# Products that nobody reads beside the attention's late units, and the norm's sums in two PSUM banks

## The chip, the cores and the metric

The kernel runs on one core of a Trainium2 chip. The metric is the device time of one execution in microseconds (us). Its engines are called by the profile's names: PE (TensorE's matmuls), PEld (TensorE's weight loads, which overlap the matmuls), DVE (VectorE), ACT (ScalarE), POOL (GpSimd) and SP (the queue that issues most DMAs).

## What is computed

One step of a one-layer encoder: a SwiGLU block, a mixer, another SwiGLU block, each followed by a layer norm. The mixer adds two branches that do not depend on each other. One is sparse attention (8 heads of 64, each query takes its 256 best keys). The other is a gated recurrence (4 heads with a 128 x 128 state), whose output is normalised by its root mean square. Cut to what matters here:

```python
S, o = lax.scan(step, S0, (q, k, v, logf))              # the recurrence, 4 heads of 128
s = einsum(q, k) * A_HEAD_DIM ** -0.5 - slopes * dist    # attention, masked to the chosen keys
o_a = einsum(softmax(s), v)
on = orec * lax.rsqrt(mean(square(orec), -1) + RMS_EPS) * gn     # the norm over each head
ob = on * silu(bg)
mixed = (sigmoid(ga) * (o_a @ wa) + sigmoid(gb) * (ob @ wb)) @ wo
```

## The kernel before, in words

The kernel has three phases, one after the other: the first SwiGLU block with the index search and the projections (to about 1460 us), `mixers` (to about 1777 us) and `back` (output projections, second SwiGLU block, last norm). Between them all engines meet at a barrier. The change is in `mixers` alone.

In `mixers` the attention is cut into units: 10 blocks of queries by 8 heads give 80 units. A unit has three steps on TensorE. `scores` ("S") multiplies the queries with the keys into one of two banks `ps_s`, in pieces of at most 512 keys. `turn` ("T") transposes the softmax weights into one of two banks `ps_t`, four tiles of 128 keys to a bank. `values` ("V") multiplies them with the values. Between S and T, VectorE takes the maximum (L2028) and ScalarE the exponential (L1934), and between T and V ScalarE copies the turned weights out of PSUM (L1949, L1953). "X" (`turn_out`) turns the output of a finished block. The later blocks have more keys: 656, 784, 912 and 1040 for the last four.

The order of all this is one list, `order`, made by `pass_order`, and every engine walks it (ScalarE with S put behind T). S runs two units ahead of T (`LOOK = 2`). The recurrence's steps ("k", "v", "u", "a", "o"; 14 of each) are dealt out between the units of the first 62% of the list. Its state product "u" writes the bank `ps_u`, which VectorE adds to the state, with `sum_done` counting. After the last step of the recurrence comes its norm, four heads. For each: "q" squares the output (ScalarE), "n" sums the squares over partitions by a product with a matrix of 1/128 (TensorE, L1914, three chunks of 384, 384 and 304 columns) and takes the root (ScalarE, L1989), "r" takes the reciprocal and multiplies (VectorE, L2082 and L2084, one chunk each), and "g" multiplies with the gate (VectorE, L2088).

PSUM has 8 banks, and all are in use: two `ps_s`, two `ps_t`, `ps_o`, and three `ps_n`. The recurrence uses these last three as `ps_kv`, `ps_ao` and `ps_u`; `ps_u` is `ps_n[2]`. In the norm, chunk i of each head uses `ps_n[i]`.

In the list, the last "u" stands at position 222. From the first S behind position 228 (the scores of unit 51) there follow 29 S, 31 T, 32 V, 4 n and 5 X.

Of the kernel before, what the change touches and what calls it, by code (L numbers as in the profile page):

```python
# [19 lines left out]
ACT = mybir.ActivationFunctionType  # L20
AX = mybir.AxisListType

P = 128
# [1682 lines left out]
def mixers(c, dram):  # L1706
# [14 lines left out]
    for b in [0, 1, "meta", "s"] + list(range(2, NB)):  # L1721
# [4 lines left out]
        else:  # L1726
            at, keys = SCORE_AT[b]
# [5 lines left out]
    order = pass_order(len(blocks), Recurrence.NRT)  # L1733
# [15 lines left out]
    with ExitStack() as st:  # L1749
# [9 lines left out]
        v_tok, k_hi, k_lo = c.v_tok, c.ka_hi, c.ka_lo  # L1759
# [10 lines left out]
        peak, peak_s, bias = sb("peak", [P, 2, 3]), sb("peak_s", [P, 2, 3]), sb("bias", [P, 2])  # L1770
# [10 lines left out]
        gn, eps, ones = sb("gn", [P, BH]), sb("eps", [P, 1]), sb("ones", [P, P])  # L1781
# [4 lines left out]
        r = Recurrence(c, dram, c.decay, ps_n, sb)  # L1786
# [9 lines left out]
        with nc.Block() as block:  # L1796
# [19 lines left out]
            @block.tensor  # L1816
            def _(pe):
                def cache():
                    pe.wait_ge(cache_in, 32)
                    for m, (src, dst, rows) in enumerate(prep):  # L1820
                        if m >= 2:
                            pe.wait_ge(kv_done, m - 1)
                        pe.transpose(ps_t[m % 2][0:rows, 0:P], src, c.ident[:]).then_inc(kv_mm, 1)

                def scores(n):
                    b, h = units[n]
                    q0, m, keys, prompt, _ = blocks[b]
                    hi, lo = (k_hi, k_lo) if prompt else (ks_hi, ks_lo)
                    if h == 0:
                        pe.wait_ge(crossed, 2 * b + 2)  # L1830
                        if not prompt:
                            pe.wait_ge(k_crossed, 4)
                    for i, (k0, w) in enumerate(pieces(keys)):
                        x = piece_at[n] + i
                        if x >= 2:
                            pe.wait_ge(peak_done, x - 1)

                        product_stacked(pe, ps_s[x % 2][:, 0:w], stack[:, b % 2, h, :], hi[:, h // 4, k0:k0 + w],
                                        lo[:, h // 4, k0:k0 + w]).then_inc(s_mm, 1)

                def turn(n):
                    b, h = units[n]
                    m, keys = blocks[b][1], blocks[b][2]
                    pe.wait_ge(exp_done, n + 1)
                    if n == 0:
                        pe.wait_ge(kv_done, len(prep) + 1)
                    tiles = (keys + P - 1) // P
                    for j, k in enumerate(range(0, tiles, 4)):
                        x = turn_at["T", n] + j
                        if x >= 2:  # L1850
                            pe.wait_ge(t_done, x - 1)
                        for i in range(k, min(k + 4, tiles)):
                            r = min(P, keys - i * P)
                            mm = pe.transpose(ps_t[x % 2][0:r, (i - k) * QB:(i - k) * QB + m],
                                              prob[0:m, n % (LOOK + 1), i * P:i * P + r], c.ident[0:m, 0:m])
                        mm.then_inc(t_mm, 1)

                def values(n):
                    b, h = units[n]
                    q0, m, keys, prompt, _ = blocks[b]  # L1860
                    tiles = (keys + P - 1) // P
                    if h == 0 and b >= 1:
                        pe.wait_ge(otok_done, b)
                    vt = v_tok if prompt else cv_tok
                    kv = slice(DH * (h // 4), DH * (h // 4) + DH)
                    for i in range(tiles):
                        if i % 4 == 0:
                            pe.wait_ge(t_done, turn_at["T", n] + i // 4 + 1)
                        r = min(P, keys - i * P)
                        mm = pe.matmul(ps_o[0:m, h * DH:(h + 1) * DH], prob_t[0:r, n % 2, i, 0:m], vt[0:r, i, kv],  # L1870
                                       start=i == 0, stop=i == tiles - 1)
                    mm.then_inc(o_mm, 1)

                def turn_out(b):
                    m = blocks[b][1]
                    x = turn_at["X", b]
                    pe.wait_ge(otok_done, b + 1)
                    pe.wait_ge(t_done, x - 1)
                    for j in range(4):
                        mm = pe.transpose(ps_t[x % 2][:, j * QB:j * QB + m], o_tok[0:m, j * P:(j + 1) * P], c.ident[0:m, 0:m])  # L1880
                    mm.then_inc(t_mm, 1)

                for what, n in order:
                    if what == "c":
                        cache()
                    elif what == "k":
                        r.turn_keys(pe, n)
                    elif what == "v":
                        r.turn_values(pe, n)
                    elif what == "u":  # L1890
                        r.update(pe, n)
                    elif what == "a":
                        r.attend(pe, n)
                    elif what == "o":
                        r.read(pe, n)
                    elif what == "S":
                        scores(n)
                    elif what == "T":
                        turn(n)
                    elif what == "V":  # L1900
                        values(n)
                    elif what == "X":
                        turn_out(n)
                    elif what == "n":
                        if n == 0:
                            pe.wait_ge(cst, 2)
                            pe.wait_ge(r.out_done, r.NRT)
                            pe.wait_ge(r.vtok_done, r.NRT)
                            pe.wait_ge(r.sum_done, r.NRT)
                        for i, (t0, w) in enumerate(CHUNKS):  # L1910
                            pe.wait_ge(sq_done, 3 * n + i + 1)
                            if n >= 1:
                                pe.wait_ge(rms_done, 3 * n + i - 2)
                            pe.matmul(ps_n[i][:, 0:w], ones[:], sq[:, i, 0:w], start=True, stop=True).then_inc(r_mm, 1)  # L1914

            @block.scalar
            def _(act):
# [38 lines left out]
                for what, n in act_order(order):  # L1956
                    if what == "k":
                        r.keep_keys(act, n)
                    elif what == "v":
                        r.keep_values(act, n)  # L1960
                    elif what == "q":
                        for i, (t0, w) in enumerate(CHUNKS):
                            if n == 0:
                                act.wait_ge(r.out_done, r.NRT)
                            else:
                                act.wait_ge(r_mm, 3 * n + i - 2)
                            act.activation(sq[:, i, 0:w], rq[:, n, t0:t0 + w], ACT.Square).then_inc(sq_done, 1)
                    elif what == "Q":
                        make_stack(n)
                        if n == 1:  # L1970
                            act.wait_ge(kv_done, len(prep) + 1)
                            for g_ in range(2):
                                act.activation(ks_hi[halves[g_], g_, :], ks_t[halves[g_], :], ACT.Copy).then_inc(khi_done, 1)
                    elif what == "S":
                        softmax(n)
                    elif what == "T":
                        keep_turned(n)
                    elif what == "X":
                        q0, m = blocks[n][0:2]
                        x = turn_at["X", n]  # L1980
                        act.wait_ge(t_mm, x + 1)
                        act.activation(c.aq[:, :, q0:q0 + m], ps_t[x % 2][:].rearrange("p (j q) -> p j q", j=4)[:, :, 0:m],
                                       ACT.Copy).then_inc(t_done, 1)
                    elif what == "n":
                        for i, (t0, w) in enumerate(CHUNKS):
                            act.wait_ge(r_mm, 3 * n + i + 1)
                            if n >= 1:
                                act.wait_ge(on_done, 3 * n + i - 2)
                            act.activation(rms[:, i, 0:w], ps_n[i][:, 0:w], ACT.Sqrt, bias=eps[:]).then_inc(rms_done, 1)  # L1989

            @block.vector
            def _(dve):
# [503 lines left out]
```

## Time and profile before

| | us |
|---|---|
| median of 3 runs | 2855.16 (2853.48 to 2855.99) |
| the profiled execution | 2865.82, its span 2864.1 |
| PE busy in the span | 2702.6 (94%) |
| PEld busy | 2611.5 (91%) |
| DVE, ACT, POOL busy | 1351.5, 695.7, 466.4 |
| mean granted clock of TensorE | 0.967 of 2.4 GHz |

PE's busy time counts matmuls whose ends are modelled and overlap, so the start-to-start times of a timeline tell more of its pace than the durations do. The last matmul of unit 79 ends at 1775.0 us of the span and the phase's last instruction, the copy behind the last X, at 1776.7.

### The profile page before, as it was taken

Reading aid. Unit: us, or ns where it says so; the run is one execution under the profiler, and the core shown is the slowest. Engines: PE = TensorE matmul, PEld = TensorE weight load, DVE = VectorE, ACT = ScalarE, POOL = GpSimd, SP = SyncE. Lnnn points to the kernel's source line nnn. Section 1 sums busy time; section 2 is a strip of 40 time slices with the busy share of each in tenths; the row PEclk is TensorE's granted clock in tenths of the full one; section 3 lists DMA queues with packets and bytes.
Section 4 is the critical chain, followed back from the end, with each engine's and each line's share of the span. In section 5 each row is a group of like instructions: output and inputs, shape, how many; then the busy total and the mean of one; then the engine's idle time right before and its main releaser. Section 6 shows DMA issues by size and latency. Waiting matters only on the chain. (4 is left out here: it accounts for less than half of the span.)

```text
span 2864.1 us, 41380 instructions
## 1 busy us (share of the span) xinstructions
PE 2702.6 (94%) x16384; PEld 2611.5 (91%) x16384; DVE 1351.5 (47%) x2834; ACT 695.7 (24%) x1162; POOL 466.4 (16%) x151
## 2 busy tenths in 40 slices
PE   8999999999987899999989997899999999999996
PEld 7999999999977789999978986898799999999995
DVE  3333333333353679999436664555633333333336
ACT  3111111111044443222525664101511111111102
POOL 1211111111110011222100000211121111111112
PEclk9999999999998899999999978999999999999998
DMA  4111111111012012222230001521011111111101
GB/s 150 45 44 44 44 44 44 44 44 44 17 37 69 20 30 52 91 94 65 76 108 2 8 1 46 174 90 39 30 59 44 44 44 44 44 44 44 44 15 61
DMA packets 144811, 149.11 MB, mean 52 GB/s; under 512 B 20240, under 2 KB 131440, under 8 KB 144576
## 3 DMA queue, kind: packets, MB, share of 16 engines
q1 hardware_dynamic: 141248, 134.45, 15.3%
q10 hardware_dynamic: 3456, 13.17, 1.1%
q8 instruction: 75, 1.23, 0.2%
q14 instruction: 32, 0.26, 0.0%
HBM read 123.82 MB, written 23.79 MB: 52 GB/s over the span
## 5 line engine op out<-in xcount | busy, mean ns | idle before, releaser
L477 DVE TENSOR_TENSOR ffn_prod<-ffn_gate,ffn_psu 128x384 f32<-128x384 f32 x132 | 69.5, 526 | 798.5 <-ACT ffn_gate L387 793.7
L67 PE MATMUL ixp_ps<-h_hi,ixp_hi 128*128 128x384 f32 (+1 forms) x1032 | 342.8, 332 | 29.0 <-ACT y L879 11.5
L387 ACT ACTIVATE ffn_gate<-ffn_psg 128x384 f32<-128x384 f32 x132 | 61.8, 468 | 1258.5 <-PE ffn_psu L69 1258.5
L67 PE MATMUL ffn_psd<-ffn_hid_hi,ffn_dn_hi 128*128 128x384 f32 (+1 forms) x1056 | 354.5, 336 | 12.7 <-DVE y L502 10.9
L502 DVE TENSOR_TENSOR y<-y,ffn_psd 128x384 f32<-128x384 f32 (+1 forms) x480 | 250.9, 526 | 218.1 <-PE ffn_psd L69 218.1
L67 PE MATMUL ffn_psg<-h_hi,ffn_up_hi 128*128 128x384 f32 (+1 forms) x1056 | 345.7, 327 | 8.2 <-DVE ffn_up_lo L402 6.5
L69 PE MATMUL ffn_psd<-ffn_hid_hi,ffn_dn_lo 128*128 128x384 f32 (+1 forms) x1056 | 344.1, 326 | 0.0
L68 PE MATMUL ffn_psd<-ffn_hid_lo,ffn_dn_hi 128*128 128x384 f32 (+1 forms) x1056 | 344.1, 326 | 0.0
L67 PE MATMUL ffn_psu<-h_hi,ffn_up_hi 128*128 128x384 f32 (+1 forms) x1056 | 344.0, 326 | 0.0
L68 PE MATMUL ffn_psg<-h_lo,ffn_up_hi 128*128 128x384 f32 (+1 forms) x1056 | 343.2, 325 | 0.0
L69 PE MATMUL ffn_psu<-h_hi,ffn_up_lo 128*128 128x384 f32 (+1 forms) x1056 | 343.0, 325 | 0.0
L69 PE MATMUL ffn_psg<-h_hi,ffn_up_lo 128*128 128x384 f32 (+1 forms) x1056 | 342.5, 324 | 0.0
L68 PE MATMUL ffn_psu<-h_lo,ffn_up_hi 128*128 128x384 f32 (+1 forms) x1056 | 342.1, 324 | 0.0
L68 PE MATMUL ixp_ps<-h_lo,ixp_hi 128*128 128x384 f32 (+1 forms) x1032 | 340.0, 329 | 0.0
L69 PE MATMUL ixp_ps<-h_hi,ixp_lo 128*128 128x384 f32 (+1 forms) x1032 | 339.0, 328 | 0.0
L406 POOL TENSOR_TENSOR ffn_dn_lo<-ffn_dn_raw,ffn_dn_hi 128x2048 fp32r<-128x2048 f32 x22 | 101.7, 4624 | 911.8 <-ACT ffn_dn_hi L380 911.8
L402 POOL TENSOR_TENSOR ffn_up_lo<-ffn_up_raw,ffn_up_hi 128x2048 fp32r<-128x2048 f32 x42 | 194.3, 4628 | 332.1 <-ACT ffn_up_hi L374 332.1
L67 PEld LDWEIGHTS ixp_ps<-h_hi,ixp_hi 128*128 128x128 f32 x1032 | 197.8, 192 | 30.9 <-issue 22.0
L67 PEld LDWEIGHTS ffn_psd<-ffn_hid_hi,ffn_dn_hi 128*128 128x128 f32 x1056 | 198.7, 188 | 28.4 <-DVE y L502 18.3
L67 PEld LDWEIGHTS ffn_psg<-h_hi,ffn_up_hi 128*128 128x128 f32 x1056 | 198.7, 188 | 9.1 <-DVE ffn_up_lo L402 6.7
L860 POOL TENSOR_TENSOR ixp_lo<-ixp_raw,ixp_hi 128x1024 fp32r<-128x1024 f32 x43 | 106.5, 2479 | 589.0 <-ACT ixp_hi L855 589.0
L68 PEld LDWEIGHTS ffn_psd<-ffn_hid_lo,ffn_dn_hi 128*128 128x128 f32 x1056 | 199.5, 189 | 0.3
(302 smaller groups left out, 4955.2 us busy)
## 6 DMA issues: line engine op xcount, KB each, us to landing
ffn_dn_raw<-in_ffn_wd SPq DMA_DIRECT2D x22, 1024.0 KB, 4.8
ffn_up_raw<-in_ffn_wg SPq DMA_DIRECT2D x20, 1024.0 KB, 5.4
ffn_up_raw<-in_ffn_wu SPq DMA_DIRECT2D x20, 1024.0 KB, 7.8
ixp_raw<-in_w_in SPq DMA_DIRECT2D x39, 512.0 KB, 3.8
spill<-y ACTq DMA_DIRECT2D x15, 536.0 KB, 2.7
mo_sig<-spill SPq DMA_DIRECT2D x32, 192.0 KB, 4.0
spill<-ix_stage ACTq DMA_DIRECT2D x9, 536.0 KB, 2.7
y<-y_spill SPq DMA_DIRECT2D x1, 4288.0 KB, 15.1
```

Of the source, the lines that this page charges most:

```text
L67: pe.matmul(out, w_hi, x_hi, start=first, stop=False)
L68: pe.matmul(out, w_hi, x_lo, start=False, stop=False)
L69: return pe.matmul(out, w_lo, x_hi, start=False, stop=last)
L387: act.activation(self.gate[:, k % 2, 0:w], self.ps_gate[k % banks][:, 0:w], ACT.Silu).then_inc(self.silu_done, 1)
L402: eng.tensor_tensor(self.up_lo[:, j], self.up_view(j), self.up_hi[:, j].bitcast(F32), ALU.subtract).then_inc(self.up_lo_done, 1)
L406: pool.tensor_tensor(self.dn_lo[:], self.dn_raw[:], self.dn_hi[:].bitcast(F32), ALU.subtract).then_inc(self.dn_lo_done, 1)
L477: dve.tensor_tensor(self.prod[:, k % 2, 0:w], self.gate[:, k % 2, 0:w], self.ps_up[k % banks][:, 0:w], ALU.mult).then_inc(self.prod_done, 1)
L502: dve.tensor_tensor(y, y, self.ps_dn[o % 2][:, 0:w], ALU.add).then_inc(self.y_done, 1)
L860: pool.tensor_tensor(self.lo[b], self.raw[:, n % 2], self.hi[b].bitcast(F32), ALU.subtract).then_inc(self.lo_done, 1)
```

## The change

Behind the recurrence, each S and each T of the attention gets three products ahead of it: 128 x 128 weights and 512 columns out of the keys, written into the recurrence's bank `ps_u`, which nobody reads any more. This holds for list positions above 228: 29 S and 31 T, so 60 times three products. The first seven of the 60 also wait until VectorE has read the last state product. The bank is thereby taken from the norm, whose chunks now use `ps_n[0]` and `ps_n[1]` in turn: chunk x waits until ScalarE's root of chunk x - 2 is done, where it had waited for chunk x - 3.

```diff
-                for what, n in order:
+                last_update = order.index(("u", r.NRT - 1))
+
+                def keep_warm():
+
+                    for _ in range(3):
+                        pe.matmul(r.ps_u[:], k_hi[:, 0, 0:P], k_hi[:, 0, 0:512], start=True, stop=True)
+
+                for at, (what, n) in enumerate(order):
+                    if at > last_update + 6 and what in "ST":
+                        if at < last_update + 20:
+                            pe.wait_ge(r.sum_done, r.NRT)
+                        keep_warm()
                     if what == "c":
                         cache()
...
                         for i, (t0, w) in enumerate(CHUNKS):
-                            pe.wait_ge(sq_done, 3 * n + i + 1)
-                            if n >= 1:
-                                pe.wait_ge(rms_done, 3 * n + i - 2)
-                            pe.matmul(ps_n[i][:, 0:w], ones[:], sq[:, i, 0:w], start=True, stop=True).then_inc(r_mm, 1)
+                            x = 3 * n + i
+                            pe.wait_ge(sq_done, x + 1)
+                            if x >= 2:
+                                pe.wait_ge(rms_done, x - 1)
+                            pe.matmul(ps_n[x % 2][:, 0:w], ones[:], sq[:, i, 0:w], start=True, stop=True).then_inc(r_mm, 1)
...
-                            act.activation(rms[:, i, 0:w], ps_n[i][:, 0:w], ACT.Sqrt, bias=eps[:]).then_inc(rms_done, 1)
+                            act.activation(rms[:, i, 0:w], ps_n[(3 * n + i) % 2][:, 0:w], ACT.Sqrt, bias=eps[:]).then_inc(rms_done, 1)
```

## Rows read from the trace of the kernel before

**Rows 1.** The page: the clock granted to TensorE in 40 slices of 71.6 us.

```profile
PEclk9999999999998899999999978999999999999998
```

**Rows 2.** Windows behind the recurrence: stretch, length, busy PE PEld DVE ACT POOL, clock, DMA.

```profile
1616.45:1655.50 39.05, 36.67 (x255) 32.44 (x255) 30.94 (x82) 30.32 (x68) 0.00 (x0) 1.00 0.00 1
1655.50:1675.80 20.30, 20.00 (x82) 18.07 (x81) 10.97 (x29) 8.57 (x22) 0.00 (x0) 0.50 0.00 1
...
1699.60:1709.70 10.10, 10.10 (x36) 8.49 (x37) 2.12 (x10) 5.66 (x14) 0.00 (x0) 0.50 0.01 2
...
1723.30:1726.90 3.60, 3.60 (x18) 3.46 (x19) 3.09 (x8) 1.78 (x4) 0.00 (x0) 0.53 0.00 0
...
1736.50:1746.50 10.00, 9.77 (x45) 8.40 (x42) 2.35 (x12) 3.26 (x7) 0.00 (x0) 0.53 0.00 0
...
1616.45:1772.80 156.35, 143.07 (x870) 125.37 (x870) 87.81 (x238) 88.94 (x191) 0.00 (x0) 0.86 0.00 1
```

**Rows 3.** TensorE's waits in that stretch: who for whom, us, times, longest.

```profile
PEld mx_s L809 <- DVE mx_peak L2028: 13.7, 16, 2.1
PE mx_s L809 <- DVE mx_peak L2028: 9.9, 13, 1.8
PE mx_t L1854 <- ACT mx_prob_t L1949: 1.5, 6, 0.3
PE mx_t L1854 <- ACT aq L1982: 1.5, 3, 0.7
```

**Rows 4.** Timeline of PE at full clock, units of 784 keys: start us, us, instruction.

```profile
1649.00 0.44 PE L809 MATMUL mx_s<-ka_hi,mx_stack 128*128 128x392 f32 x1
...
1652.66 0.63 PE L1880 MATMUL mx_t<-ident,mx_o_tok 128*128 128x128 f32 x4 [0.27 <-ACT mx_prob_t L1949]
```

**Rows 5.** The same at half clock: one whole cycle of a unit.

```profile
1660.26 0.69 PE L809 MATMUL mx_s<-ka_hi,mx_stack 128*128 128x392 f32 x1
...
1666.43 0.69 PE L809 MATMUL mx_s<-ka_hi,mx_stack 128*128 128x392 f32 x1
```

**Rows 6.** Timeline of PE, full clock: three 456-column products, then the turn.

```profile
1679.55 0.37 PE L810 MATMUL mx_s<-ka_lo,mx_stack 128*128 128x456 f32 x1
...
1680.17 0.93 PE L1854 MATMUL mx_t<-ident,mx_prob 128*128 128x128 f32 x7
```

**Rows 7.** Timeline of DVE: one unit's cycle with a piece of the norm.

```profile
1626.19 2.55 DVE L2082 RECIPROCAL y<-y 128x384 f32<-128x384 f32 x1
...
1630.35 2.55 DVE L2082 RECIPROCAL y<-y 128x384 f32<-128x384 f32 x1
```

**Rows 8.** Timelines of PE and ACT: norm sums and the roots that follow, four heads.

```profile
1620.70 1.97 PE L1914 MATMUL mx_n<-y,mx_ones 128*128 128x384 f32 x6
1624.18 1.46 ACT L1989 ACTIVATE y<-mx_n,mx_eps 128x384 f32<-128x384 f32 x3
...
1643.88 2.07 PE L1914 MATMUL mx_n<-y,mx_ones 128*128 128x384 f32 x6
1646.04 1.46 ACT L1989 ACTIVATE y<-mx_n,mx_eps 128x384 f32<-128x384 f32 x3
...
1675.70 1.97 PE L1914 MATMUL mx_n<-y,mx_ones 128*128 128x384 f32 x6
1678.78 1.46 ACT L1989 ACTIVATE y<-mx_n,mx_eps 128x384 f32<-128x384 f32 x3
...
1707.49 3.09 PE L1914 MATMUL mx_n<-y,mx_ones 128*128 128x384 f32 x6
1710.72 1.46 ACT L1989 ACTIVATE y<-mx_n,mx_eps 128x384 f32<-128x384 f32 x3
```

**Rows 9.** Timeline of PE, last block: waits inside S and T; the longest wait.

```profile
1735.92 0.43 PE L809 MATMUL mx_s<-ka_hi,mx_stack 128*128 128x344 f32 x1 [1.82 <-DVE mx_peak L2028]
...
1761.40 0.42 PE L809 MATMUL mx_s<-ka_hi,mx_stack 128*128 128x344 f32 x1 [0.45 <-DVE mx_peak L2028]
...
1763.10 0.28 PE L1854 MATMUL mx_t<-ident,mx_prob 128*16 128x128 f32 x1 [0.25 <-ACT mx_prob_t L1949]
```

## The prediction

> **What bounds the kernel now.** I read the views in this order: the page for where TensorE's clock is low, windows of the stretch that the change touches, the waits in it, and then timelines of single units for start-to-start times. The page shows a dip of the clock in slices 22 to 26, behind the recurrence [rows 1]. The windows cut that stretch, 1616.45 to 1772.8 us, where the clock changes [rows 2]. Four spells at half clock (1.2 of 2.4 GHz) stand in it: 20.3, 10.1, 3.6 and 10.0 us, 44.0 us together. TensorE is the busiest engine there by far: 143.1 of 156.35 us, against 87.8 for VectorE and 88.9 for ScalarE. Its own waits are short [rows 3]. By the matmul rows they come to 9.9 + 1.5 + 1.5 = 12.9 us; the weight loads see more of the same waits, 13.7 us for the largest against 9.9, and with the smaller ones about 22 us. I take 17.5 us of waits, the middle of the two. So the stretch is TensorE's: about 17.5 us of waiting, about 20 us lost to the half clock (next paragraph), and some 119 us of work at full clock. What is put on TensorE here is paid for, except where it falls into a wait.
>
> **What the half clock costs now.** A unit of 784 keys that waits for nothing takes 1652.66 - 0.27 - 1649.00 = 3.39 us at full clock [rows 4] and 1666.43 - 1660.26 = 6.17 us at half clock [rows 5]. Of each microsecond at half clock (6.17 - 3.39) / 6.17 = 0.45 is lost, so the four spells lose 44.0 x 0.45 = 19.8 us. If the products hold the clock, that comes back. Its bounds are 22 us, half of all 44.0, above, and zero below, if the clock falls as often as before.
>
> **Part 1, the products.** 29 S and 31 T get three products each, 180 of 512 columns, in the number format of the score products. Three score products of 456 columns take 1680.17 - 1679.55 = 0.62 us start to start, 0.207 each [rows 6]. By columns, 512 take 0.207 x 512 / 456 = 0.232 us, so 180 take 41.8 us. Part of a product's time may be a fixed charge: at 1 column per cycle of 2.4 GHz, 512 columns are 0.213 us, which gives 38.4 us as the lower end. At half clock a product would take twice as long. I take 41.8. No engine waits for them and they wait for nothing but, in the first seven groups, VectorE's read of the last state product. The phase's list has it nine or more places earlier, so it is long done; I put that wait at nothing, and it would cost under 1 us once.
>
> **What of it is hidden.** A group of three (0.70 us) stands ahead of the waits of an S or a T and fills them. What it can't fill are waits inside an S or a T. In the last block a unit's scores have three pieces for two banks, so the third waits for VectorE, 0.45 us, and the ninth tile's turn waits for ScalarE's copy, 0.25 us [rows 9]. Eight units of both make 5.6 us, and I leave 1 us for others. Of the 17.5 us of waits 10.9 are then filled. At most 17.5 could be; at the least 12.9 - 6.6 = 6.3. Could VectorE rather than TensorE set the pace, so that more is free? A unit with a piece of the norm takes VectorE 1630.35 - 1626.19 = 4.16 us, reciprocal to reciprocal [rows 7], more than TensorE's 3.39 us for a unit of 784 keys or, by keys, 2.85 us for one of 656. That is why S waits for `mx_peak`. But there are 12 such pieces to 29 units, the scores run two units ahead, and VectorE has 68 us of the stretch free. With two groups of products, 1.4 us more per unit, TensorE is at 4.25 us for 656 keys and at more for the later blocks, and is the slower one in each.
>
> The Trainium skill (Perfetto Trace Analysis, Identifying the Most-Contended Engine) says that matmul busy time is a bad measure of TensorE's headroom and that the busy share of LDWEIGHTS is a good one. By the weight loads' busy time, TensorE has 156.35 - 125.4 = 31.0 us free here, not 17.5 [rows 2]. The first spell speaks against it: the matmuls leave 0.3 of its 20.3 us free, the loads 2.2, so part of the gaps between loads is no room for work. It is a rival below.
>
> **Part 2, the norm in two banks.** The third sum of a head now waits for the first one's root, and everything behind it on TensorE (the next V, X or S, and the products) waits with it. Before, it waited for a root of the head before, long done. The roots come late because ScalarE first copies the turned weights, does an exponential and loads a table. For the four heads the sums start at 1620.70, 1643.88, 1675.70 and 1707.49, and the rows of three roots start at 1624.18, 1646.04, 1678.78 and 1710.72 [rows 8]. The first root ends 0.57 us behind its start (three in 1.46 us), that is 4.05, 2.73, 3.65 and 3.80 us behind the sums' start; the third sum would have started 1.2 us behind it. That leaves stalls of 2.85, 1.53, 2.45 and 2.60 us, 9.4 in all. Since TensorE bounds the stretch, they are paid. If the following waits shrink by it, perhaps half: 5 us is the lower end. ScalarE has no backlog there, so the upper end is near, 12 us. Later pieces of the norm move nothing else: VectorE needs the sums several units later.
>
> **The clock around these stalls.** The longest wait for `mx_peak`, 1.82 us, ends at 1735.9 [rows 9], and a spell begins at 1736.5 [rows 2]. The stalls of 1.5 to 2.9 us are about as long, so I expect the clock to fall behind each of the four. The spells should be short, since the products are wide: two of the old spells ended at 1675.8 and 1709.7, while the wide norm sums of 1675.70 and 1707.49 ran [rows 2, 8]. The shortest spell was 3.6 us, which cost 1.6 us. I take four at 1.5 us, 6 us; bounds 0 and 15 us. The Trainium skill (TensorE: Matmul & The Clock Gate, A second HAM failure mode: psum-queue depth-cycling) tells of just this: short idles between matmul groups that cycle through PSUM banks make the clock swing. That speaks for the products and against the two-bank norm; what it would cost comes out as in the 6 us above.
>
> **The sum.** Products +41.8, clock back -19.8, waits filled -10.9, norm stalls +9.4, new spells +6.0: +26.5 us on the profiled execution, so its span goes from 2864.1 to 2890.6 us, with 1.7 us around it 2892.3. The profiled execution before (2865.8) stands 10.7 us above the median 2855.2; I carry the difference over, which gives 2881.7, so 2882 us. What lies behind the phase starts from a barrier with idle engines, before and after, and doesn't change.
>
> **The rivals.**
> *The pace is set by VectorE and ScalarE, not by TensorE.* Then the products are free, the clock comes back, and the stalls fall into slack as well: 2855.2 - 19.8 + 0 to 9 gives 2835 to 2844 us, faster. This decides once VectorE's chain takes over 4.3 us in nearly every unit. For it speaks the 4.16 us of the units with a norm piece [rows 7], against it that these are 12 of 29, and VectorE's 87.8 us of 156.35 [rows 2].
> *The clock isn't held.* The clock falls beside the products too, or the stalls bring it down each time; then the change doesn't do what its first half says. The 19.8 us stay lost, without the 6 us: +41.8 - 10.9 + 9.4 = +40.3, so 2896 us. For it: the clock fell at 1655.5 although TensorE had been busy 36.7 of the 39.05 us before [rows 2]. Against it: wide products ended two spells.
> *More slack than the matmul rows show.* With the loads' 31.0 us as the slack, 31.0 - 6.6 = 24.4 are filled: +41.8 - 19.8 - 24.4 + 9.4 + 6.0 = +13.0, 2868 us. If the products are at their lower end (38.4), the stalls at 5 and no new spell comes, it is -0.8, 2854 us: no change.
>
> **Chances.** My forecast 60%, clock not held 13%, more slack 20% (of which 10 at its low end, within 0.2%), VectorE's pace 7%. What a measurement can tell from no change is about 0.2%, 5.7 us. Faster by over that 0.07, within it 0.10, slower 0.83. The forecast's own range is 2866 to 2892 us. For 8 in 10 I take 2858 to 2897: it holds the third rival but its low end, and the clock rival; left out are faster, most of no change, and some above.
>
> **What would show it.** 180 new matmuls of 128x512, 0.23 us apart. PEclk 1.0 in most of the stretch, short dips behind the norm's sums. A wait of PE ahead of the norm's third sum for ScalarE's root, four times, 1.5 to 3 us. The waits of S for `mx_peak` shrunk from 9.9 to some 4 us, all inside units of the last block. Unit 79's values ending near 1801 us instead of 1775. I am wrong if the four stalls are missing, if S still waits between units (then VectorE has the pace), or if the half clock lasts over 30 us.

## The result, and the profile after

The changed kernel takes 2912.84 us in the median of its first 4 runs (2894.65 to 2919.51), against 2855.57 us (2853.48 to 2856.73) for the kernel before: 1.0182 times as long, 95% interval 1.0145 to 1.0218. Twelve more runs, in two sets of six, gave medians of 2899.23 and 2898.58 us, with ratios of 1.0149 (1.0112 to 1.0186) and 1.0143 (1.0099 to 1.0186). Over all 16 runs the median is 2899.6 us, some 44 us above the kernel before: 11 of them lie from 2892 to 2901 us and 5 from 2912 to 2921, and three of the first four were of the upper five. The forecast was 2882 us, in a range of 2858 to 2897 us. The direction was right, the size too small, and the measured time lies outside the range.

The page of the changed kernel: its span and the clock in 40 slices of 72.8 us. The span was 2864.1 us before.

```profile
span 2910.9 us, 41741 instructions
PEclk9999999999998999999987999999999999999997
```

The windows of the changed kernel (length, busy PE PEld DVE ACT POOL, clock, DMA): the stretch behind the recurrence, where before [rows 2] shows it by its pieces; four spells in it; and a spell of 37.4 us ahead of it.

```profile
1631.78:1821.99 190.21, 175.57 (x1067) 150.80 (x1066) 88.42 (x238) 88.81 (x191) 0.00 (x0) 0.95 0.00 1
...
1632.50:1635.60 3.10, 3.10 (x11) 2.54 (x10) 1.97 (x8) 0.00 (x0) 0.00 (x0) 0.52 0.00 0
1645.10:1649.10 4.00, 4.00 (x19) 3.47 (x19) 0.00 (x0) 0.91 (x2) 0.00 (x0) 0.58 0.00 0
1710.20:1714.00 3.80, 3.80 (x12) 3.08 (x12) 1.27 (x5) 0.00 (x0) 0.00 (x0) 0.55 0.00 0
1744.80:1754.60 9.80, 9.80 (x33) 8.33 (x34) 2.59 (x7) 0.70 (x2) 0.00 (x0) 0.50 0.01 2
...
1529.80:1567.20 37.40, 37.40 (x190) 30.49 (x188) 16.23 (x61) 11.91 (x45) 0.00 (x0) 0.50 0.00 1
```

The stretch is cut in every kernel in the same way: from unit 51's first score product (or the new product ahead of it) to the end of unit 79's values. Before, that is 1616.45 to 1775.05, 158.6 us; the end of rows 2 at 1772.8 lay inside unit 79's values. After, it takes 190.2 us: 31.6 more. It also begins 15.3 us later, because of the spell at 1529.8 to 1567.2 us. That spell is in the recurrence, in instructions that the change leaves as they were, while TensorE waits for nothing (PE busy 37.40 of 37.40). Behind the stretch, both profiles take 1089 us to their ends.

TensorE's waits in the stretch, changed kernel, beside [rows 3] of before (who for whom, us, times, longest):

```profile
PE mx_n L1926 <- ACT y L2001: 8.1, 4, 2.5
PE mx_s L809 <- DVE mx_peak L2040: 4.6, 8, 1.1
PE mx_t L1854 <- ACT mx_prob_t L1961: 2.0, 8, 0.3
```

The wait of the norm's third sum for ScalarE's root is new: four times, 8.1 us. The waits of S for VectorE fell from 9.9 us (13 times) to 4.6 us (8 times, one in each unit of the last block), and those behind an X are gone.

The timeline of PE, changed kernel: one unit with its two groups of products, and the sums of the third head with the wait in them.

```profile
1669.71 0.96 PE L1888 MATMUL mx_n<-ka_hi 128*128 128x512 f32 x3
1670.51 0.34 PE L809 MATMUL mx_s<-ka_hi,mx_stack 128*128 128x392 f32 x1
...
1671.22 0.86 PE L1888 MATMUL mx_n<-ka_hi 128*128 128x512 f32 x3
1671.92 0.93 PE L1854 MATMUL mx_t<-ident,mx_prob 128*128 128x128 f32 x7
...
1704.04 1.46 PE L1926 MATMUL mx_n<-y,mx_ones 128*128 128x384 f32 x4
1707.99 0.75 PE L1926 MATMUL mx_n<-y,mx_ones 128*128 128x304 f32 x2 [2.50 <-ACT y L2001]
```

Three products take 1671.92 - 1671.22 = 0.70 us between the unit's scores and its turn. Nothing overlaps them. From the first of them to the end of the turn the unit takes 1672.68 - 1669.71 = 2.97 us, where the unit of [rows 4] took 1650.58 - 1649.00 = 1.58 for the same scores and turn; the difference is 1.39 us for six products, 0.232 each. (Five of the 60 groups also wait for VectorE's last read of the state product, not seven as said above; no such wait shows in the profile.)

### The profile page after: what moved, and what is told of

It reads as the page before. It is cut to its first block and busy times, and to the rows that moved or that the text cites. A ratio compares the mean times of both kernels' runs of the same rounds, so it can differ in the third digit from the quotient of the medians.

```text
span 2910.9 us, 41741 instructions
## 1 busy us (share of the span) xinstructions
PE 2748.9 (94%) x16564; PEld 2647.8 (91%) x16564; DVE 1350.4 (46%) x2834; ACT 696.2 (24%) x1162; POOL 466.3 (16%) x151
## 3 DMA queue, kind: packets, MB, share of 16 engines
q1 hardware_dynamic: 141248, 134.45, 14.9%
## 5 line engine op out<-in xcount | busy, mean ns | idle before, releaser
L67 PE MATMUL ffn_psd<-ffn_hid_hi,ffn_dn_hi 128*128 128x384 f32 (+1 forms) x1056 | 354.7, 336 | 12.7 <-DVE y L502 10.9
```

The source lines that it names most:

```text
L67: pe.matmul(out, w_hi, x_hi, start=first, stop=False)
```

## One account for all profiles

To compare kernels I take the stretch apart in the same way each time: its length L, TensorE's waits by its matmul rows, the time at half clock H (2 x (1 - mean clock) x L) of which 0.45 is lost [rows 4, 5], and the products at 0.232 us each. What is left should be TensorE's own work at full clock, the same in every kernel. The windows give the clock with two digits, so H is known to about 1.6 us and 0.45 H to 0.7.

| kernel | products | L | waits | H | 0.45 H | products' time | left |
|---|---|---|---|---|---|---|---|
| before, first profile | 0 | 158.6 | 13.2 | 44.4 | 20.0 | 0 | 125.4 |
| before, second | 0 | 151.4 | 11.7 | 33.3 | 15.0 | 0 | 124.7 |
| before, third | 0 | 151.1 | 11.9 | 30.2 | 13.6 | 0 | 125.6 |
| changed, first | 180 | 190.2 | 14.7 | 19.0 | 8.6 | 41.8 | 125.1 |
| changed, second | 180 | 191.7 | 14.7 | 23.0 | 10.4 | 41.8 | 124.8 |
| changed, third | 180 | 193.2 | 14.7 | 27.1 | 12.2 | 41.8 | 124.5 |
| two banks, no products | 0 | 167.0 | 18.8 | 46.8 | 21.1 | 0 | 127.1 |
| third sum later | 180 | 175.9 | 8.9 | 3.5 | 1.6 | 41.8 | 123.6 |
| same, one product each | 60 | 152.7 | 11.9 | 3.1 | 1.4 | 13.9 | 125.5 |
| same, one before S | 29 | 148.1 | 13.5 | 3.0 | 1.4 | 6.7 | 126.5 |
| same, every second S | 15 | 156.7 | 14.0 | 31.3 | 14.1 | 3.5 | 125.1 |
| same, no products | 0 | 151.4 | 14.9 | 24.2 | 10.9 | 0 | 125.6 |
| products behind the norm | 42 | 163.5 | 13.2 | 32.7 | 14.7 | 9.7 | 125.9 |

The rest is 125.4 us within 1.8 us, over lengths from 148 to 193 us. So the stretch is TensorE's throughout, and the work, the waits, the half clock and the products account for it to within those 1.8 us. (The kernel with products of 128 columns is left out, since their time was not measured apart.)

## The experiments

### The changed kernel and the kernel before, again

No edit; the changed kernel a second time:

> The changed kernel once more, unaltered, with more timings. Its profile had two parts: +31.6 us in the stretch behind the recurrence (where the change is) and +15.3 us ahead of it, from a spell at half clock at 1529 to 1568 us, in code that the change leaves as it was. Theory A (the spell is not tied to the change; it falls or doesn't by small differences in time): the runs spread over some 20 to 25 us, part of them near 2895, and the kernel before shows such a spell in some run too. Theory B (the change brings it in every run): all runs at 2910 or above, the kernel before within 3 us. In either case the stretch from unit 51's first product to unit 79's last takes 190 us (+31 to +32).

Measured: six runs from 2892.12 to 2915.65 us, median 2899.23; 23 runs of the kernel before beside them from 2848.18 to 2876.26, median 2854.97. The profile (2897.1 us) has no early spell, and its stretch takes 191.7 us:

```profile
1615.09:1806.81 191.72, 177.09 (x1067) 152.36 (x1066) 88.42 (x238) 88.74 (x191) 0.00 (x0) 0.94 0.00 1
```

So the 15 us ahead of the stretch are not part of every execution: theory B, as written, is out.

The kernel before for a second and a third profile:

> The kernel before, unaltered, for a second profile. Its runs went from 2848 to 2876 us, the profiled one at 2865.8 in their upper part. Theory A: the spells at half clock differ from execution to execution, in place and length, so this profile has another amount of half clock behind the recurrence than 44.4 us, and the stretch of 158.6 us changes by 0.45 us for each us of it. If the median run (2855) differs from the first profile by spells in the stretch, a run near 2855 has some 20 us less half clock there and a stretch near 149 us. Rival: 44 us of half clock and 158 us again, the differences lie elsewhere.

> The kernel before once more, for a third profile: the same expectation. Stretch between 140 us (no half clock) and 165 us, span in line with it: the rest of the span varies by less than 5 us, unless a spell falls into the recurrence as in the changed kernel's first profile.

Measured: medians of 2854.27 us (10 runs, 2845.86 to 2869.18) and one run of 2853.74 us, profiles of 2852.4 and 2852.0 us. Windows of the stretch in the two:

```profile
1614.78:1766.19 151.41, 139.72 (x887) 123.80 (x886) 87.65 (x238) 89.01 (x191) 0.00 (x0) 0.89 0.00 1
```

```profile
1614.00:1765.11 151.11, 139.20 (x887) 122.18 (x886) 87.72 (x238) 88.92 (x191) 0.00 (x0) 0.90 0.00 1
```

Half clock is there in both, but 30 and 33 us of it instead of 44, and the stretch is 7.3 us shorter. I had looked for 20 us less and 149 us; it is 11 to 14 us less and 151 us, the remaining 4.5 us of the difference between the profiles lying outside the stretch. The profile from which I predicted was not typical of its kernel: it held more half clock than a run at the median. Not all of it moves about, though. The longest wait for `mx_peak`, 1.8 us, stands in all three profiles of before, and a spell of 10.2 us begins within 1.3 us behind it in each (at 1737.0, 1728.2 and 1727.0).

The changed kernel a third time:

> The changed kernel a third time, for the spread. So far ten executions: six from 2892 to 2901 and four from 2912 to 2920, and one of the four has a profile, with a spell of 39 us in the recurrence, ahead of the change, that cost 17 us. If that early spell is what separates the two groups, this profile shows it when its time is above 2910 and not when it is below 2902. The stretch behind the recurrence again 190 to 193 us with 19 to 23 us of half clock, in spells behind the norm's waits. If the upper group comes as often as in the kernel before (there three of 29 at 2875), it is chance: one or two of the executions.

Measured: 2892.05 to 2900.94 us in five runs, and 2921.24 in the sixth. The profile is of a run at 2900.94, without an early spell, stretch 193.2 us and 27.1 us of half clock, a little above what I had written. The clock is recorded for every run, profiled or not: over the whole execution it was 0.963 to 0.966 in the five runs of the upper group and 0.970 to 0.974 in the other eleven. So the upper group holds more half clock; where, only the one profile shows.

### The norm in two banks alone

```diff
-                        keep_warm()
+                        pass
```

(and without the wait for `sum_done` ahead of it)

> The norm in two banks alone, without the products. If the third sum's wait is paid by TensorE in full, as I say, the four waits come to 8 to 9.4 us and the stretch of 158.6 us becomes 167 to 169, more if the waits bring the clock down. The rival (a pace set by VectorE and ScalarE) says that the waits fall into slack: under +3 us. Theory B of the spell ahead of the stretch needs the products or their bytes in the program; this kernel has as many instructions for TensorE as before, so B gives no early spell and 2862 to 2868 us, while A allows one.

Measured: 2869.57 us, ratio 1.0054 (1.0032 to 1.0075): 15 us slower than before, and no early spell in its profile. Its stretch, and its two longest kinds of wait:

```profile
1614.47:1781.49 167.02, 148.14 (x887) 128.88 (x886) 88.01 (x238) 89.26 (x191) 0.00 (x0) 0.86 0.00 1
```

```profile
PE mx_s L809 <- DVE mx_peak L2038: 7.8, 12, 1.8
PE mx_n L1924 <- ACT y L1999: 7.6, 4, 2.6
```

The stretch takes 167.0 us, which is within what I expected, but against the 151.3 us of the two later profiles of before it is 15.7 us. Of these, 7.6 are the waits, and (46.8 - 31.8) x 0.45 = 6.8 us more half clock. So the two-bank turn by itself costs as much as it makes TensorE wait, and about as much again in clock. The second half rests on single profiles, whose half clock differs by 14 us for one kernel, but the timings say the same: the medians of 12 and 23 runs lie 14.6 us apart, and the clock over the whole execution is 0.9675 in the median against 0.970. Three of the 12 runs lie from 2882 to 2884 us, 12 to 15 us above their median, so there are such runs without any products too. The rival by which VectorE and ScalarE set the pace, and waits are free, falls.

### The third sum later

```diff
+                    if late is not None and what in "SV":
+                        norm_sum(late, 2)
+                        late = None
...
+                        norm_sum(n, 0)
+                        norm_sum(n, 1)
+                        late = n
```

(`norm_sum` holds the body of the loop over chunks; all 180 products stay)

> The changed kernel, but each head's third norm sum is issued one S or V later, so that this work lies in the wait for ScalarE's root. My account: of the 8.1 us of these waits some 2 us stay, and with them go most of the half-clock time that followed them in the changed kernel, worth 6 to 9 us; the stretch takes 175 to 178 us instead of 190. The rival that the clock falls for another reason gives 184 (waits gone, spells there).

Measured: 2882.46 us, ratio 1.0083 (1.0053 to 1.0114), profile 2877.7. Its stretch and its waits in the norm:

```profile
1615.19:1791.06 175.87, 166.94 (x1067) 144.85 (x1066) 88.38 (x238) 88.61 (x191) 0.00 (x0) 0.99 0.00 1
```

```profile
PE mx_n L1896 <- ACT y L2010: 2.3, 3, 0.9
```

The waits fall by 5.8 us and the half clock from 19 to 27 us down to 3.5, a single spell at the start of the stretch (1615.7 to 1619.1). A spell begins there in every profile but the first of before. The stretch is 14 to 17 us shorter than in the three profiles of the changed kernel. That shows by experiment what I had only argued: the other spells of the changed kernel follow the norm's waits. Timed runs bear it out: the clock over the whole execution is 0.974 to 0.976 in all six of this kernel, against 0.963 to 0.974 in the 16 of the changed one.

### Fewer products

From the kernel above, with one product in each group:

```diff
-                    for _ in range(3):
+                    for _ in range(1):
```

> As the kernel whose third norm sum comes later, but one product ahead of each S and T instead of three: 60 instead of 180. Its stretch took 175.9 us with 3.5 us of half clock. 120 products fewer save 120 x 0.233 = 28 us. If one product is enough to hold the clock, the stretch takes 148 us, and up to 6 us more as waits are less filled: 148 to 154. If the clock falls as in the kernel before (some 40 us of half clock), 18 us more: 166 to 172. The number tells how much of the gain in clock can be had for less.

And one ahead of each S, none ahead of T:

```diff
-                    if at > last_update + 6 and what in "ST":
+                    if at > last_update + 6 and what == "S":
```

> The same with one product ahead of each S alone, 29 in all, 6.8 us of products. If the clock is held: stretch 141 to 148 us and a time some 5 us below the kernel before. If not (the more likely, as this is near the kernel before): 44 us of half clock, 158.6 + 6.8 - 4 of waits filled + 2 of norm waits = 163 us, and 2858 to 2862.

Measured: 2859.29 us, ratio 1.0011 (0.9992 to 1.003), stretch 152.7 us; and 2857.45 us, ratio 1.0014 (0.9995 to 1.0033), stretch 148.1 us. The windows of the second:

```profile
1616.62:1764.73 148.11, 134.39 (x916) 116.67 (x915) 87.76 (x238) 88.91 (x191) 0.00 (x0) 0.99 0.00 1
```

A sixth of the products holds the clock as well as all of them: 3.0 and 3.1 us at half clock beside 3.5, which is in each of the three profiles the same one spell of 3.4 us at the start of the stretch. I had thought that unlikely for 29. Its waits of 1.37 and 1.58 us for VectorE are followed by no spell, unlike the wait of 1.8 us in the profiles of before. The stretch is 3 us shorter than a median run's of before. But over the whole kernel nothing of it can be measured: the interval holds 1, and the 5 us that I had expected did not come. Outside the stretch its profile is 4.8 us longer than the two at the median of before, and why is not shown.

The control, with the later third sum and no product at all (edit as for the two banks alone):

> The control for the two before: the third norm sum one S or V later, two banks, and no products at all. The kernels with 180, 60 and 29 products have 3.5, 3.1 and 3.0 us of half clock. If the products hold the clock, half clock comes back here, 30 to 44 us, and the stretch takes 124.5 + 13 of waits + 2.4 of the norm's + 14 to 20 = 154 to 160 us. If it was the moved sum that holds it, there is under 5 us of half clock and a stretch of 141 to 143.

Measured: 2859.49 us, the runs against those of before 0.9993 (0.9969 to 1.0017). The windows of its stretch:

```profile
1616.96:1768.78 151.82, 136.46 (x887) 119.57 (x886) 87.87 (x240) 89.11 (x191) 0.00 (x0) 0.92 0.00 1
```

24.2 us at half clock in the stretch (which ends at 1768.39; the window is 0.4 us longer): less than I had written (30 to 44), but seven times what the kernels with 29, 60 and 180 products have, and the stretch, 151.4 us, is under what I expected (154 to 160). So it is the products that hold the clock, and not the moved sum.

Two cheaper ones: a product of 128 columns ahead of each S, and one of 512 ahead of every second S.

```diff
-                        pe.matmul(r.ps_u[:], k_hi[:, 0, 0:P], k_hi[:, 0, 0:512], start=True, stop=True)
+                        pe.matmul(r.ps_u[:, 0:P], k_hi[:, 0, 0:P], k_hi[:, 0, 0:P], start=True, stop=True)
```

> One product of 128 columns instead of 512 ahead of each S: 29 x some 0.1 us = 3 us instead of 7. If the count of filled waits is what matters, the clock holds and the stretch takes 144 to 145 us, the time 2851 to 2853, a little under the kernel before. If the columns matter, a quarter of them is too few: half clock of 20 to 40 us and a stretch of 153 to 160.

```diff
-                    if at > last_update + 6 and what == "S":
+                    if at > last_update + 6 and what == "S" and n % 2:
```

> One product of 512 columns ahead of every second S, 15 in all, 3.5 us. If the clock is held by so few: stretch 144 to 146 us, 2851 to 2854. If it falls between them: 20 to 40 us of half clock, stretch 153 to 160, no gain over the kernel before.

Measured: 2856.47 us (0.9991, 0.9972 to 1.0011), stretch 150.4 us with 18.0 us at half clock; and 2858.54 us (0.9999, 0.9978 to 1.002), stretch 156.7 us with 31.3. Neither holds the clock as the 29 wide ones do; the first lies between my two cases, the second in the one without a gain. These are single profiles, and the amount of half clock differs between executions of one kernel by 14 us. The clock over the whole execution, in the median of 11 or 12 runs each (6 for the 180), puts the kernels in the same order: 0.971 without products, 0.972 for either of the two cheap kinds, 0.973 with 29 wide ones, 0.975 with 60 and with 180; the kernel before has 0.970.

### Products behind the norm, three banks

```diff
+                    if at > last_piece and what in "ST":
+                        pe.wait_ge(rms_done, 3 * BH)
+                        keep_warm()
```

(on the kernel before; `last_piece` is the position of the norm's last "r")

> The norm keeps its three banks, and only the S and T behind its last piece get the products: 14 groups, 42 products. At 0.233 us each they cost 9.8 us. They fill waits of about 2 us outside the pieces and give back what the last spell of half clock (10.0 us) costs, some 4.5 us: the stretch +2 to +4 us, so 2857 to 2860. If products were free beside the attention, 2849 to 2851; if they don't hold the clock, 2863.

Measured: 2861.88 us, ratio 1.002 (0.9994 to 1.0046), stretch 163.5 us. That is more than I expected: 4.9 us over the first profile of before and 12 over the other two, where I had written 2 to 4. The windows ahead of the first product and from it on:

```profile
1615.29:1726.00 110.71, 102.90 (x614) 90.42 (x613) 75.77 (x187) 71.26 (x154) 0.00 (x0) 0.85 0.00 1
1726.00:1778.78 52.78, 47.44 (x317) 40.30 (x316) 11.94 (x51) 17.31 (x37) 0.00 (x0) 1.00 0.00 1
```

The clock is 1.00 from the first product to the end, and 0.85 ahead of it, so the spell of 10.2 us that all three profiles of before have in this part is gone. It had cost 10.2 x 0.45 = 4.6 us, and the products cost 9.7.

## Why the prediction was wrong

The step that failed is the one by which a gain in clock, read out of one profile 10.7 us above its kernel's median, was carried over to the median whole. It wasn't the only term that was off. The forecast was +26.5 us on a median of 2855.2. The 16 runs say some +44, of which +40.4 are in the stretch. There, 5.5 us are clock that wasn't there to come back (14.3 instead of 19.8), 5.7 are waits that weren't filled (5.2 instead of 10.9), 4.4 are the spells of the changed kernel (10.4 instead of 6.0), and -1.3 the norm's waits (8.1 instead of 9.4). Some 4 us lie outside the stretch. That the median of the first four runs is another 13 us higher is the upper group, of which the prediction knew nothing: it had no term for what lies ahead of the stretch.

**What bounds the stretch**: right. TensorE does, and all profiles add up to the same 125 us of work. Before I had put it at 119 us, because of the next point.

**The waits now and what is filled of them**: mis-sized, by as much as the term that failed. I took 17.5 us, the middle between the matmul rows (12.9) and the weight loads (22), and let 10.9 of it be filled. The sum over the profiles closes with the matmul rows alone. Filled were 13.2 - 6.6 = 6.6 us in the first profile, next to the lower end that I had given (6.3), and 11.8 - 6.6 = 5.2 against the two at the median. That is 4.3 to 5.7 us too much. The rival built on the page Perfetto Trace Analysis of the Trainium skill (Identifying the Most-Contended Engine) took the slack by the weight loads, 31.0 us. By this account it was further off still: such gaps between loads are no room for products in this stretch.

**The products' price**: right. 0.232 us each, 41.8 us in all, paid in full.

**The norm in two banks**: nearly right. Four waits of 8.1 us in place of 9.4, of 2.29, 0.77, 2.50 and 2.50 us. The second head's was half of what I had, since ScalarE was less behind: its first root started 1.60 us behind the sums (1675.80 - 1674.20) instead of 2.16.

**The clock around these waits**: right in kind, too small. I expected four spells that cost 6 us. They came behind the three long waits (1645.1, 1710.2 and 1744.8 us), not behind the one of 0.77 us, and so in all three profiles; one more, of 3.4 us, stands at the start of the stretch, ahead of any wait of the norm. Half clock of 19.0, 23.0 and 27.1 us in three profiles cost 8.6, 10.4 and 12.2 us, 10.4 in the mean. The Trainium skill (TensorE: Matmul & The Clock Gate, A second HAM failure mode: psum-queue depth-cycling) tells of short idles between groups of matmuls, with PSUM banks in turn, that make the clock go up and down. The trace agrees: with the third sum later the spells behind these waits go (3.5 us are left of 19 to 27).

That the spells would be short I had in part from a misreading. Of the two old spells that I took to have ended in a wide norm sum, the first was over before the sum started at 1675.70; the clock is whole from there on, and 0.73 already from 1675.50 to 1675.70:

```profile
1675.70:1675.90 0.20, 0.20 (x3) 0.19 (x2) 0.00 (x0) 0.20 (x2) 0.00 (x0) 1.00 0.00 0
```

Only the second (1709.7, in the sum of 1707.49) is as I said.

**The clock that comes back**: the step that failed. I sized it at 19.8 us from one profile, and then took the profiled execution's 10.7 us above the median as something that stays the same on both sides. It was no such constant. The two later profiles of before, at 2853.7 and 2854.1 us, hold 30 and 33 us of half clock, which cost 14.3 us in the mean. So in a median run there were 14.3 us to win and not 19.8, and the rest of the 10.7 us was chance elsewhere in that execution. The changed kernel's median has no such excess taken off: its profiles of runs at 2898.8 and 2900.9 us are the ones near its median.

For the first profile against the first my terms, put right, give +41.8 - 20.0 - 6.6 + 8.1 + 8.6 = +31.9 us, where the stretch grew by 31.6 and my sum had 26.5. For a median run it is +41.8 - 14.3 - 5.2 + 8.1 + 10.4 = +40.8 us (waits 11.8 before, 6.6 and 8.1 after), and the stretch measured 191.7 - 151.3 = +40.4. The remaining 4 us or so to the 44 of the medians lie outside the stretch, where single profiles differ by as much: from its end on, 1086.2 to 1089.1 us in the three profiles of before and 1088.9 to 1090.3 in the three of the changed kernel. Whether part of that belongs to the change is not shown.

**What stays open.** 5 of 16 runs of the changed kernel lie 12 to 21 us above the others. One of them was profiled, and there it was the spell in the recurrence: at half clock for 37.4 us, it delayed unit 51 by 15.3 us. The kernel before has such runs too (of the 90 that ran beside the experiments 11 lie 12 us or more above the median, 7 of them between 2872 and 2879 us), but none of these was profiled, and whether the change makes them more frequent is not shown. Nothing ahead of the spell is changed in TensorE's order. Three of the first four runs lay in the upper group, which is why the first median is 2912.84.

**The rivals.** VectorE's pace: out, by the two-bank kernel and by the account. More slack: out, 5.2 to 6.6 us were filled and not 24.4. The clock not held: its first case, that the clock falls beside the products too, is out, since 3 us of half clock are left where the norm doesn't make TensorE wait. Its second, that the stalls bring it down each time, is half of what happened: 19 to 27 us of half clock remain of 30 to 33, so only 14.3 - 10.4 = 3.9 us of clock came back, and over the whole execution the clock is 0.970 in the median with and without the change. The rival's +40.3 us stands next to the measured +40.4, but partly by luck: it had 5.7 us too much for the waits filled, and gave nothing for the clock that came back.

## What to carry to other kernels

Products put on the engine that sets the pace are paid for one by one, so use the fewest that hold the clock: here 29 did as well as 180, and even they only paid for themselves. When a bank is taken from one step for another, price the new wait twice, once as a wait and once as the half clock behind it (7.6 and 6.8 us here). And before a gain in clock is read out of one profile, look how far that execution lies above its kernel's median: such an excess may be part of the very thing that is to be won, and a median run has that much less to give.

## What the runs showed of the hardware

The half clock in one and the same stretch of one and the same kernel took 44.4, 33.3 and 30.2 us in three executions, for the most part in other places each time; only the 10.2 us behind the longest wait, of 1.8 us, came in all three. A spell of 37.4 us came while TensorE had work without a gap, in one of the three profiled executions of the changed kernel; the 29.7 us before it (1500.0 to 1529.7) had been without a gap as well, at a clock of 1.00. And 29 products of 512 columns, 6.7 us of work, went with 3.0 us of half clock in the stretch, against 24.2 us without them and 18.0 us with products of 128 columns.
